# The recurrent stage of a two-block kernel: pair products of equal weights joined, and the first product of each level on block-diagonal weights

## What is computed

```python
def rwkv_scan(s0, r, decay, k, v, kk, a, reverse, emit):
    def step(s, inp):
        w_t, k_t, v_t, kk_t, a_t = inp[:5]
        s_kk = jnp.einsum('bhvk,bhk->bhv', s, kk_t)
        s = (s * w_t[:, :, None, :]
             - s_kk[..., None] * (kk_t * a_t)[:, :, None, :]
             + v_t[..., None] * k_t[:, :, None, :])
        y = jnp.einsum('bhvk,bhk->bhv', s, inp[5]) if emit else None
        return s, y
...
    for d in range(2):
        rev = d == 1
        s_c, yc_d = rwkv_scan(s0, r_c, w_c, kd_c, v_c, kk_c, a_c, rev, emit_ctx)
        _, yx_d = rwkv_scan(s_c, r_x, w_x, kd_x, v_x, kk_x, a_x, rev, True)
        y_x = y_x + yx_d
```

## Time and profile before

| what | value |
|---|---|
| time, median of three runs | 3574.14 us (3565.3 to 3575.73) |
| profiled execution, its own time | 3563.52 us |
| its span, first to last instruction | 3561.9 us |
| mean granted clock of TensorE | 0.921 |
| TensorE, VectorE, ScalarE, POOL busy | 89%, 47%, 38%, 22% |

### The profile page before, as it was taken

One profiled execution on the slowest core, in us unless ns is written; L12 is line 12 of the kernel. 1 busy time (PEld: TensorE's weight loads), 2 busy tenths in 40 slices (PEclk: granted clock), 3 DMA queues, 4 the chain that ended last, 5 costly groups with the idle time before them and its releaser, 6 DMA issues.

```text
span 3561.9 us, 57637 instructions
## 1 busy us (share of the span) xinstructions
PE 3168.1 (89%) x22992; PEld 2352.4 (66%) x22992; DVE 1672.1 (47%) x2566; ACT 1354.7 (38%) x1767; POOL 798.4 (22%) x487
## 2 busy tenths in 40 slices
PE   7999999969976999899999899994877699599996
PEld 5887666644434887688752686774776487388885
DVE  2110155565997333311012502337766521489996
ACT  4342245553334322343212321223332222278884
POOL 4444200000004443344410222102222234200001
PEclk9999999989998999999999997556999799799998
DMA  2222511101211222222245121000000022399997
GB/s 104 94 94 89 218 53 47 47 24 64 75 62 36 95 95 89 76 93 92 88 180 204 54 71 60 24 0 10 4 5 4 2 100 93 128 377 412 411 412 274
DMA packets 106923, 397.17 MB, mean 112 GB/s; under 512 B 11680, under 2 KB 11696, under 8 KB 106240
## 3 DMA queue, kind: packets, MB, share of 16 engines
q1 hardware_dynamic: 95040, 347.42, 26.6%
q0 software_dynamic: 8400, 35.15, 2.6%
q10 hardware_dynamic: 3312, 12.06, 0.8%
HBM read 361.55 MB, written 33.03 MB: 111 GB/s over the span
## 4 chain that ended last, share of the span: by engine, by line
PE 66%; DVE 12%; issue 6%; ACT 2%; DMA 1%; POOL 1%; DVEq 1%; ACTq 0%; SPq 0%; POOLq 0%
PE psum L221 9%; PE psum L220 9%; PE psum L222 9%; PE psum L1772 6%; PE psum L2610 3%; PE psum L2611 3%; PE psum L2612 3%; PE psum L525 3%; PE psum L1430 2%; DVE mem L921 2%; PE psum L1111 2%; PE psum L533 2%; PE psum L1410 2%; PE psum L793 1%; PE psum L556 1%
## 5 line engine op out<-in xcount | busy, mean ns | idle before, releaser
L210 POOL TENSOR_TENSOR ring_r<-ring,whi 128x1024 fp32r<-128x1024 f32 x247 | 600.0, 2439 | 1019.9 <-ACT whi L205 1019.9
L205 ACT ACTIVATE whi<-ring 128x1024 fp32r<-128x1024 f32 x247 | 255.6, 1054 | 528.5 <-DMA ring<-stream 528.3
L222 PE MATMUL psum<-xn_r,whi 128*128 128x512 f32 x1024 | 406.5, 397 | 0.0
L1772 PE MATMUL psum<-mem 64*64 64x64 f32 x9664 | 251.9, 225 | 79.7 <-issue 30.8
L2547 DVE TENSOR_TENSOR er_r<-er,eh 128x1024 fp32r<-128x1024 f32 x268 | 309.4, 1218 | 1.1 <-ACT eh L2535 0.5
L220 PE MATMUL psum<-ffn_xh,ring_r 128*128 128x512 f32 x704 | 279.7, 397 | 19.0 <-DVE xn_r L233 19.0
L1772 PEld LDWEIGHTS psum<-mem 64*64 64x64 f32 x9664 | 232.3, 138 | 97.3 <-issue 51.9
L2535 ACT ACTIVATE eh<-er 128x1024 fp32r<-128x1024 f32 x268 | 268.3, 1071 | 42.4 <-DMA er<-experts 41.3
L221 PE MATMUL psum<-ffn_xh,whi 128*128 128x512 f32 x704 | 281.2, 399 | 0.0
L793 PE MATMUL psum<-xn,ring 128*128 128x512 f32 x512 | 224.6, 599 | 8.5 <-DVE mem L731 4.3
L222 PEld LDWEIGHTS psum<-xn_r,whi 128*128 128x128 f32 x1024 | 194.2, 190 | 45.6
(11 more groups left out here) (510 smaller groups left out, 6103.7 us busy)
## 6 DMA issues: line engine op xcount, KB each, us to landing
ring<-stream SPq DMA_DIRECT2D x359, 512.0 KB, 3.5
er<-experts SPq DMA_DIRECT2D x276, 512.0 KB, 8.8
xs_dram<-zero_row POOLq DMA_DIRECT2D x1, 12288.0 KB, 38.8
xs<-xs_dram SPq DMA_DIRECT2D x23, 512.0 KB, 8.3
ys_dram<-y_t ACTq DMA_DIRECT2D x23, 512.0 KB, 6.7
mem<-rpb POOLq DMA_DIRECT2D x8, 512.0 KB, 4.6
resid<-x_t SPq DMA_DIRECT2D x1, 2048.0 KB, 7.9
spill<-resid POOLq DMA_DIRECT2D x1, 2048.0 KB, 10.0
```

The source lines that it names most:

```text
L205: act.activation(WHI.get(part, whi)[:, (SLAB_AT[part] + j) % RING, :, :], w, ACT.Copy).then_inc(w_hi, 1)
L210: pool.tensor_tensor(ring_r[:, s, :, :], ring[:, s, :, :], f(WHI.get(part, whi)[:, s, :, :]), ALU.subtract).then_inc(w_lo, 1)
L222: return pe.matmul(bank, hi[:, b, :], x_lo_, start=False, stop=stop, skip_group_check=True)
L1772: ins = pe.matmul(psum[o, bank, first:first + L], lhs(n)[r], rhs(n)[r], start=i == 0 if start is None else start, stop=i == len(terms) - 1 ...
```

## The change

Five things are done. AT with R2, and CT with R1, have the same weights (bt and kt): kap and rho now lie in one buffer `kr`, and one product runs 128 columns over both (`pair_B`, `pair_K`; 64 columns if the chunk doesn't emit), into banks 4 and 5, one for each direction. ScalarE copies AT into a buffer of twice the size as two diagonal blocks of 64x64 for each head pair; the other blocks are cleared once by POOL. `level_Y` is one product with 128x128 weights for two heads, not two of 64x64. The order on TensorE, VectorE and ScalarE is rearranged accordingly: A goes beside W4, bT and the two K groups stand alone. Some waits are bound to other semaphores.

```diff
-        kap, rho = [take(W8, "b") for _ in range(3)], [take(W8, "b") for _ in range(3)]
+        kr = [take(2 * W8, "b") for _ in range(3)]
+        kap, rho = [v[:, 0:W8] for v in kr], [v[:, W8:2 * W8] for v in kr]
...
-        AT = [take(W8, "a") for _ in range(2)]
+        AT = [take(2 * W8, "a") for _ in range(2)]
...
+            for v in AT:
+                pool.memset(v, 0.0).then_inc(rz, 1)
...
+            def decay_products(c):
+                act.wait_ge(pe_m.sem, pe_m.at(c, "B1"))
+                for a in range(2):
+                    r = slice(64 * a, 64 * a + 64)
+                    act.activation(AT[c % 2][r].rearrange("p (d b u t) -> p d b u t", d=2, b=4, u=2)[:, :, :, a, :],
+                                   psum[r, 4:6, 0:4 * L].rearrange("p d (b t) -> p d b t", b=4), ACT.Copy).then_inc(act_m.sem, 1)
...
+            def with_both(n, bank, lhs, c):
+                cols = 2 if emits(c) else 1
+                for h in range(2):
+                    r, o = ROWS[h], ROWS[h ^ 1]
+                    ins = pe.matmul(psum[o, bank, :].rearrange("p (w q t) -> p w q t", w=2, q=4)[:, 0:cols, n % 4, :],
+                                    tile_(lhs, n)[r], kr[c % 3].rearrange("p (w n t) -> p w n t", w=2, n=8)[r, 0:cols, n, :],
+                                    start=True, stop=True, skip_group_check=True)
+                return ins
...
             def level_Y(c, l, d):
...
-                return lambda n: tiles(n, d, (ALONG, of(AT[c % 2]), X_of(c)), at=n % 4 * L)
+                return lambda m: pe.matmul(psum[:, d, m % 4 * L:(m % 4 + 1) * L], AT[c % 2][:, m * P:(m + 1) * P], X_of(c)(m),
+                                           start=True, stop=True)
...
-                if more:
-                    beside(w, ALL, pe_l, pair_AT(n), ALL, pe_m)
-                    w = level_W(c, 2, 1)
-                    beside(w, ALL, pe_l, pair_A(n), ALL, pe_m)
-                    level_Ys(c, 3, pair_CT(n), pe_m)
...
+                for d in range(2):
+                    w = level_W(c, 2, d)
+                    if more:
+                        beside(w, ALL, pe_l, pair_B(n, d), HALF[d], pe_m)
+                    else:
+                        alone(w, ALL, pe_l)
+                level_Ys(c, 3)
...
-                if r:
-                    level_Ys(c, 5, pair_R1(n), pe_m)
-                else:
-                    level_Ys(c, 5)
...
+                if more:
+                    alone(pair_bT(n), ALL, pe_m)
+                level_Ys(c, 5)
+                for d in range(2):
+                    if more:
+                        alone(pair_K(n, d), HALF[d], pe_m)
+                    alone(level_W(c, 5, d), HIGH, pe_l)
```

More of the change, by code:

```diff
@@ L1535, in hybrid_block_kernel @@
         kT, bT, vt = ([take(W8, "b") for _ in range(2)] for _ in range(3))
-        st = [take(W8, "a") for _ in range(2)]
+        st = [take(W8, "b") for _ in range(2)]
         Ym, Gs, Us = take(W8, "a"), take(W8, "a"), take(W8, "a")
@@ L1714, in rwkv_act @@
             unit(0)
[L1715 removed]
+            decay_products(0)
             pair_copy(0, "kT", kT)
@@ L1811, in lora_pe, with pair_B @@
                                 ins.then_inc(pe_w.sem, 1)
[L1813 to L1819, removed]
+            def pair_B(c, d):
+                if d == 0:
+                    for e in range(2):
+                        W(dve_p, c, f"bt{e}")
+                    W(pool_p, c, "rho1" if emits(c) else "kap1")
+                    if c:
+                        W(dve_m, c - 1, "R1" if emits(c - 1) else "CT")
+                return lambda n: with_both(n, 4 + d, bt, c)
@@ L1821, in pair_A, with pair_K, pair_kT @@
+            def pair_K(c, d):
+                if d == 0:
+                    W(pool_p, c, "kt1")
+                    W(act_m, c, "AT1")
+                    W(dve_m, c, "R2" if emits(c) else "XT")
+                return lambda n: with_both(n, 4 + d, kt, c)
             def pair_A(c):
                 if c:
-                    W(act_m, c - 1, "bT")
+                    W(act_m, c - 1, "vt")
                 return lambda n: tiles(n, M_BANK["A"], (ACROSS, of(kap[c % 3]), of(bt)))
-            def pair_CT(c):
+            def pair_kT(c):
@@ L1837, in pair_bT, with pair_vt @@
+            def pair_vt(c):
                 W(dve_m, c, "X")
[L1838 to L1850, removed]
@@ L1915, in rwkv_pe @@
             lora_pe(0)
-            alone(pair_AT(0), ALL, pe_m)
-            alone(pair_A(0), ALL, pe_m)
-            alone(pair_CT(0), ALL, pe_m)
+            for d in range(2):
+                alone(pair_B(0, d), HALF[d], pe_m)
             lora_pe(1)
             alone(pair_kT(0), ALL, pe_m)
+            alone(pair_A(0), ALL, pe_m)
             alone(pair_bT(0), ALL, pe_m)
+            for d in range(2):
+                alone(pair_K(0, d), HALF[d], pe_m)
             for c in range(NCH):
                 n, s = c + 1, c - 1
-                more, last, y, r = n < NCH, c > 0, emits(s), n < NCH and emits(n)
+                more, last, y = n < NCH, c > 0, emits(s)
                 if last:
@@ L1968, in rwkv_pe @@
                 if more:
[L1969 removed]
+                    beside(w, ALL, pe_l, pair_A(n), ALL, pe_m)
                 else:
                     alone(w, ALL, pe_l)
[L1972 to L1984 removed]
+                if more:
+                    alone(pair_bT(n), ALL, pe_m)
+                level_Ys(c, 5)
+                for d in range(2):
+                    if more:
+                        alone(pair_K(n, d), HALF[d], pe_m)
+                    alone(level_W(c, 5, d), HIGH, pe_l)
             s = NCH - 1
@@ L2058, in scaled_b @@
                 if c and d == 0:
-                    wait(pe_m, c - 1, "R2" if emits(c - 1) else "bT")
+                    wait(pe_m, c - 1, "bT")
                 dve.scalar_tensor_tensor(half(bt, d), half(tb, d), -1.0, half(pinv, d), ALU.mult, ALU.mult).then_inc(dve_p.sem, 1)
@@ L2171, in rwkv_dve @@
                     state_decay(s)
+                if more:
+                    pair_X(n)
+                if more and emits(n):
+                    masked(n, "R2", R2, PP(1), M_R)
                 if next_too:
```

120 lines of the change are left out of this document (53 added, 67 removed).

## The result

The changed kernel took 3724.22 us (median of 4 runs, 3719.72 to 3734.51), the kernel before 3574.93 us (4 runs): a ratio of 1.0426, 95% interval 1.0402 to 1.0451. It is slower by about 150 us. The profiled execution has a span of 3722.1 us and a mean granted clock of 0.899; before they were 3561.9 us and 0.921.

The account below looks back on a forecast made before the run. An emitting chunk was taken to last about as long as its instructions need to arrive. Work +54 and clearings +2 us, (354 + 56)/0.85 = 482 us for the stage, +128 on 3574 gave 3702 us; range 3605 to 3770.

Parts of the forecast that it names:

- (a): The forecast case: the stage's work gets longer and its clock lower, 3702 us; chance 0.45.
- (b): Rival: the clock stays at 1.00 in the stage's middle, only the added work counts, 3630 us; chance 0.27.
- (c): Rival: changing shape costs nothing, since weights are loaded ahead, 3597 us; chance 0.11.
- (d): Rival: instruction supply is the bound and 144 fewer passes a chunk count, full pass 58 ns, 3536 us; chance 0.09.
- (f): Rival: the parts cancel, time the same within 0.3%; chance 0.03.
- (e): Rival: as (a), but the waits for VectorE stay, +168 us, 3742 us; chance 0.05.
- The change of shape: Y1 and Y4, full products alternating with quadrant products: 0.63 us for each of eight, +8.2 us a chunk for two groups.
- The clock: TensorE's granted clock over the stage: mean 0.85, stage (354 + 56)/0.85 = 482 us, +128; bounds 1.00 and 0.75.
- The three Y levels alone: Y levels without an alternating partner: +1.16 us each, +3.5 us a chunk.
- The lone groups: bT, K0 and K1, losing their partners: +0.93 us for bT and +1.8 us for K0 and K1 an emitting chunk.
- The waits vanish: TensorE's waits in the stage, 34 us for VectorE and 32.1 us without shown cause, were let vanish.
- The supply of instructions: Instruction queue in an emitting chunk: 992 passes need 28 to 29.5 us to arrive, about the chunk's 29.4 us.

Follow-up runs that it names:

- e4: Changed kernel with four full-array products followed by four of the other group, 4 changes of shape a group instead of 16: 3633.9 us, ratio 1.0173.
- e2: Changed kernel with Y levels 1 and 4 back in quadrants, full-array Y only at 2, 3 and 5, where it stands alone: 3583.8 us, ratio 1.0031.
- e3: Changed kernel with Y levels 2, 3 and 5 back in quadrants, full-array Y only at 1 and 4, where it alternates: 3700.4 us, ratio 1.0360.
- e1: Changed kernel with all Y levels back in 64x64 quadrant products, everything else as changed: 3571.7 us, ratio 1.0005 to the kernel before.
- e10: e1 with bT beside Y5 and the stage's start mended (POOL clears the block buffers last), K0 and K1 still alone: 3565.9 us, ratio 0.9980.
- e11: e1 with K0 and K1 beside the two halves of W5, bT left alone: 3582.3 us, ratio 1.0028.
- e12: Against e10, no block buffer or clearing: AT one plain copy, with joined pair products, quadrant Y, bT beside Y5, K0 and K1 alone: 3564.0 us, ratio 0.9976.
- e7: Changed kernel with full-array Y at level 1 alone, one alternating group a chunk, other levels in quadrants: 3658.1 us, ratio 1.0250.

## Why the prediction was right

3702 us was forecast in 3605 to 3770, 3724 measured; the forecast case (a) came about. Rival (b) is out by the clock, (c) by the 0.16 and 0.20 us and by the 90 us that e4 gives back, (d) by the 115 ns of a full pass, and (f), no change, by the size of the loss. (e), 3742, is as near to the measured time as (a): the waits for VectorE did stay in part. The mechanism and its two signs, 0.6 us a pair and a lower clock, are as forecast; that the sum came within 22 us is partly luck, as several terms were off in both directions.

**The price of a full-array pass.** 112 ns was taken, 115 ns measured (Y5 alone at full clock). Right. (The 58 ns of a quadrant pass divide by 16 places where there are about 15.5; 60 ns is nearer, and changes nothing.)

**The change of shape.** 0.15 and 0.20 us were read off the lora products, 0.16 and 0.20 us measured at Y5; 0.63 us for one n was the sum and 0.60 to 0.62 us is measured. The rows were of half the array's rows against a quadrant and held for the whole array as well. Here the Trainium skill's rule on changing the mode in "TensorEngine Tiling (Array Packing)", Key Properties, agrees with the trace; read as a whole pass's length for each change it would have been too high.

**The clock.** It was forecast at 0.85 from the ends of the stage and is 0.78 over the stage. Put into the prediction's own sum that is too much: (354 + 56)/0.78 = 526 us would have been +172, where the stage grew by 156. So the clock was mis-sized one way, and the division of the whole stage by it the other, since an alternating n grows by 1.03/0.62 = 1.66 and not by 2. The two offset each other in part.

**How the 156 us of the stage split** is an estimate: 0.78 over 519 us is the lower of the two levels for (1 - 0.78)/0.5 = 44% of it, 228 us. At that level an alternating n takes 1.03 against 0.62 us, and four quadrants or the lora products nearly twice. With 1.7 as the mean factor 228 us would have been 134 us, so some 94 us go to the clock, less 12 us or so that the stage lost to it before (0.96 over 355 us by the same working). The other 74 us or so are changes of shape and longer products; with a factor of 2 they would be 56 us. +54 was forecast for them, the two clearings apart.

**The three Y levels alone** were mis-sized. +1.16 us each, 42 us over twelve chunks, was forecast; e2 shows 12 us, and the step from e3 to the changed kernel 24 us. The sum counted them as pure addition, since it started from work without waits. That they filled waits is read from the waits of e2 and not tested: VectorE's in the levels (L2115 and L2107) fall from 17.3 + 10.4 us in e1 to 12.4 + 5.7 in e2.

**The lone groups** were charged with +2.7 us an emitting chunk, and in e1 the whole of them with all else costs nothing. For bT the charge fits: 0.93 us in eleven chunks is 10 us, and e10, which takes it back, is 9 us under e1. For K it was wrong: e11 shows that taking K's place away costs 8 us, because K hides VectorE's latency. Both are seen where a chunk still had waits to fill; what the lone groups cost in the changed kernel, where TensorE is busy nearly throughout, no run shows.

**The waits vanish** was right for the gaps without cause (32.1 to 1.2 us), half right for VectorE (34 to 20 us). In the one stretch at full clock 704 passes took 30 us, which makes 36.1 us for 848, not 33.2.

**The start** cost 3.7 us in the trace, not 2: the step "two clearings, 1.84 us" missed that ScalarE's wait for them, moved ahead of its first work, put a table load behind them.

**The supply of instructions**, the reason for rival (d), was read as nearly binding from two numbers that matched, 28 to 29.5 us of supply and 29.4 us of chunk. e1 shows that it wasn't alone in ending a chunk: with 6% fewer passes (928 for 992) the time is the same, and the queue slowed down. But e1 also has the lone groups; with bT beside Y5 (e10, e12) the same 928 passes give 0.2% back. How much the supply held back the kernel before stays open.

What stays open: why one alternating group a chunk (7.8 us) costs more than a second adds, since e7 has the one of Y1 and no run has the one of Y4 alone, so that the place and the number aren't told apart; and how the clock's loss divides between the pauses of a change and the smaller share of the array in use between them. No run separates these.

## What to carry to other kernels

Joining two small products into one block-diagonal one halves the instructions and not the time: a full-array pass took 115 ns where two quadrant passes side by side took some 60 ns, and it leaves no quadrant for a partner. If products of different shapes must be mixed, put them in runs: 16, 8 and 4 changes a group cost 3724, 3659 and 3634 us for the same work. And where TensorE waits for VectorE inside a chain, a group standing alone may be free (K here) while the same group put beside another lays the wait open; another (bT) is better off beside. So cost it by what it covers.

## What the runs showed of the hardware beyond that

The granted clock follows how products are ordered, not only which they are. Full-array Y products by themselves kept 1.00 with TensorE busy for 135.8 of 150 us (e2); alternating, with TensorE busy for 136.6 of 150 us, it was granted 0.80 (e3), and with 128.4 us 0.86 (e7). At the same busy share in the profile the clock was thus 1.00 or 0.80. In the changed kernel it fell from 1.00 to 0.50 inside an alternating group, with no idle time shown.

On this point the Trainium skill, "TensorE: Matmul & The Clock Gate", in its second failure mode, names brief idling between groups of matmuls, there from cycling through PSUM banks, as a cause of a clock that swings. The starts that come 0.16 to 0.20 us after the pass ahead, inside what the profile counts as busy, would fit; that they are the cause is not shown.
